# Attention loop of a hybrid decoder step on one core: projections moved ahead of the transposes in three of four steps

## The chip, the cores and the metric

The kernel is one program on one core of a Trainium2 chip. The metric is the device time of one execution in microseconds (us). The kernel before takes 2657.1 us, the median of three runs (2655.6, 2657.1, 2657.28).

TensorE (PE) multiplies matrices; its weight loads (PEld) are instructions of their own and overlap its matmuls. ScalarE (ACT) evaluates functions and copies, VectorE (DVE) does elementwise work and reductions, GpSimd (POOL) does the splitting of weights here, and SyncE (SP) issues most of the DMAs. Each engine runs its own instructions strictly in program order; the engines meet only at semaphores.

## The reference, cut to what matters

Two Griffin-style layers run over 1024 prompt tokens and 32 sample tokens (8 sequences of 4): one RG-LRU layer and one differential attention layer, each followed by a gated feed-forward block with a causal convolution. What the change touches is the attention layer, with 8 heads:

```python
kv = rmsnorm(x, kv_norm) @ w_kv                 # keys and values, also outputs
q  = (rmsnorm(x, norm_mix) @ w_q)               # per head two branches of 64
s  = einsum('bqhcd,bkhcd->bhcqk', q, k) * scale + bias   # causal, T5 bias
p  = softmax(s)
w  = p[:, :, 0] - lam * p[:, :, 1]              # difference of the two branches
o  = einsum('bhqk,bkhe->bqhe', w, v)
o  = rmsnorm(o, subln) * (1 - lam_init)
x  = x + o @ w_o
```

The sample tokens see 256 older keys and values besides, read from a paged cache.

## The kernel before, in words

All products are made as three matmuls of values split into a high and a low part, so that they keep float32 accuracy. The attention layer is one software pipeline, written out by hand: 64 **steps** `g`, which are 8 heads `h` times 8 query tiles of 128 rows (`t = g % 8`; `TILES` gives the order 0, 1, 7, 6, 2, 3, 5, 4 of the tiles). A tile `i` has `i + 1` key blocks, so steps with t = 2 and 3 are the large ones.

While a head's attention is computed, the projections (q, k, v) of the next head are made by the same engine between the pieces of attention. They are cut into **products** of three matmuls of 128x352 each (`fill`, lines 997, 999, 1001); eight products make a **chunk** (a third of the tokens of one 128-wide unit), three chunks a unit (`raw`), and nine products are done in each step. Chunks alternate between PSUM banks 0 and 1, so a chunk can start only when VectorE has taken out the chunk two before it (`raw_done`, lines 2209 and 2212). With nine products a step, a chunk begins after 6 products in the step t = 2, after 5 in t = 3, and so on down.

What TensorE does in a step, in this order:

- `scores(g)` (line 1029): query times keys of tile g, with 64-row matmuls in pairs, into banks 2 to 5; it waits until VectorE has read the scores before.
- `turn_weights(g - 2)` (line 1041): transposes of the combined softmax weights.
- `values(g - 3)` (line 1053): transposed weights times values.
- `sample_scores` in t = 0 (lines 1080, 1085) and `sample_output` in t = 4 (line 1112), both with 32-column matmuls; `sample_turn` in t = 5 (line 1121).
- `fill`, the nine products. In t = 2, 6 and 7 `ahead(g)` splits them into four and five, and between the two parts stand, in t = 2, `turn_values(h)` (lines 1065 and 1069: the values of the head turned, in three events) and `sample_weights(h)` (lines 1095, 1097), and in t = 6 and 7 `turn_output(h - 1, ...)` (line 1129).

The transposed weights, values and outputs land in PSUM banks that other engines empty. Banks 6 and 7 form a **ring**: `ring_order()` must list the events in the order in which TensorE makes them, each takes the bank of the one two before it, and has to wait for its reader (`open_event`). The weights of large tiles go to banks 3 and 5 instead (`beside_scores`), which the scores of large tiles need too: the scores in steps with g % 4 == 2 wait until the weights turned in the step before are read (`wait_weights_read`).

ScalarE does in a step: `weights_back(g - 2)` (line 1594, takes the turned weights out of PSUM), in t = 2 `values_out(h)` (issues the DMA of the values at line 1573 and takes the turned values out, lines 1576 and 1582), `exponentials(g)` (1603), `square_sum(g - 4)` (1612); in t = 4 `deviation(h - 1)` (1618, a square root, with a load of its table), `high_qk` (1542) and `sample_queries` (1556); at the head of t = 5 `sample_back(h)` (1665), whose result `sample_turn` waits for; at the head of t = 3 `sample_second(h)` (1654).

VectorE does in a step: `biased(g)` (2244: adds the bias, finds the minima), `output_rows(g - 3)` (2228, takes the result of `values(g - 3)` out of its ring bank), the chunks that are done, `combine(g - 1)` (2257, 2258, 2260), and in some steps the sample's operations. After the loop comes a tail written out by hand: the last heads' products end at step 56, steps 60 to 63 begin the output projection (`project`), and then `squares` (line 1180) follows in the ring.

Of the kernel before, what the change touches and what calls it, by code (L numbers as in the profile page):

```python
# [169 lines left out]
def filled(g):  # L170

    return LEAD if g < 0 else FIRST if g == 0 else min(16 + RATE * (g + 1), PRODUCTS)
# [4 lines left out]
    return (filled(g) - filled(g - 1)) // 3  # L177


def ahead(g):  # L180

    n = filled(g) - filled(g - 1)
    return n // 2 if g % 8 in (2, 6, 7) else 0


def beside_scores(g):

    return halves(g) == 2 and g < STEPS - 2
# [7 lines left out]
def ring_order():  # L196

    order = []
    for g in range(STEPS + 3):
        h, t = divmod(g, 8)  # L200
        if 2 <= g < STEPS + 2:
            order += [("w", g - 2, b) for b in range(halves(g - 2))]
        if g >= 3:
            order.append(("o", g - 3))
        if g < STEPS and t in (0, 4, 5):
            order.append((("scores", h), None, None, None, ("output", h), ("turned", h))[t])
        if g < STEPS and t == 2:
            order += [("v", h, 0), ("v", h, 1), ("v", h, 2), ("weights", h)]
        if g < STEPS and h and t >= 6:
            order.append(("ot", h - 1, t - 6))  # L210
        if g == STEPS - 1:
            order.append(("squares",))
    return order + [("ot", NH - 1, 0), ("ot", NH - 1, 1)]
# [33 lines left out]
def program(nc, I, O, S):  # L247
# [5 lines left out]
    with ExitStack() as ctx:  # L253
# [543 lines left out]
        def _(pe):  # L797
# [187 lines left out]
            def fill(n):  # L985

                for j in range(pos[0], min(pos[0] + n, PRODUCTS)):
                    q, k = divmod(j, KT)
                    m, c = divmod(q, NCH)
                    if j == 0:  # L990
                        wait_read(pe, A_A)
                    if q >= 2 and k == 0:
                        pe.wait_ge(raw_done, q - 1)
                    if c == 0 and k == 0:
                        pe.wait_ge(w_lo, U_A + 2 + m + 1)
                    s, cols = (U_A + m) % 2, slice(c * CH, (c + 1) * CH)
                    pe.matmul(PS[:, q % 2, 0:CH], WHI[:, s, k, :], XNH[:, k, cols],  # L997
                              start=(k == 0), stop=False)
                    pe.matmul(PS[:, q % 2, 0:CH], WLO[:, s, k, :], XNH[:, k, cols],  # L999
                              start=False, stop=False)  # L1000
                    last = pe.matmul(PS[:, q % 2, 0:CH], WHI[:, s, k, :], XNL[:, k, cols],  # L1001
                                     start=False, stop=(k == KT - 1))
                    if k == KT - 1:
                        last.then_inc(chunk_done, 1)
                pos[0] = min(pos[0] + n, PRODUCTS)
# [7 lines left out]
            def scores(g):  # L1013
                h, t = divmod(g, 8)
                i, p = tile_of(g), h % 2
                n = (i + 1) * P
                if g >= 4 and g % 4 == 2:

                    wait_weights_read(pe, g - 3)
                if t == 0:  # L1020
                    pe.wait_ge(qkl_done, 2 * h + 2)
                if g:
                    pe.wait_ge(ttr_done, 2 * g)
                for b in range(0, n, 512):
                    w = min(512, n - b)
                    for j, (q, k) in enumerate(((QHI, KHI), (QLO, KHI), (QHI, KLO))):
                        for c in range(2):
                            rows = slice(c * HD, (c + 1) * HD)
                            last = pe.matmul(PS[:, 2 + 2 * c + b // 512, 0:w],  # L1029
                                             q[p][rows, i * P:(i + 1) * P], k[p][rows, b:b + w],  # L1030
                                             start=(j == 0), stop=(j == 2))
                            if j == 2 and b + w == n:
                                last.then_inc(s_done, 1)
# [90 lines left out]
            def turn_output(h, half):  # L1124

                pe.wait_ge(on_done, h + 1)
                z = open_event("ot", h, half)
                for b in range(4):
                    last = pe.transpose(PS[:, z, b * P:(b + 1) * P], OQ[:, h % 2, 4 * half + b, :],
                                        IDENT[:, :])  # L1130
                last.then_inc(ev_done, 1)
# [22 lines left out]
            for g in range(STEPS):  # L1154
                h, t = divmod(g, 8)
                scores(g)
                if g >= 2:
                    turn_weights(g - 2)
                if g >= 3:
                    values(g - 3)  # L1160
                if t == 0:
                    sample_scores(h)
                if t == 4:
                    sample_output(h)
                if t == 5:
                    sample_turn(h)
                fill(ahead(g))
                if t == 2:
                    turn_values(h)
                    sample_weights(h)  # L1170
                if h and t >= 6:
                    turn_output(h - 1, t - 6)
                fill(filled(g) - filled(g - 1) - ahead(g))
                if g == STEPS - 4:
                    pe.wait_ge(raw_done, PRODUCTS // KT)
                if g >= STEPS - 4:
                    project(g - (STEPS - 4), 0, (0, 1))
            pe.wait_ge(sosq_done, 1)
            z = open_event("squares")
            pe.matmul(PS[:, z, 0:NH * TS], ONES[:, :], OSQ[:, :, :].rearrange("p h t -> p (h t)"),  # L1180
# [98 lines left out]
        def _(act):  # L1279
# [398 lines left out]
            for g in range(STEPS):  # L1678
                h, t = divmod(g, 8)
                if 0 < h < NH - 1 and t == 7:  # L1680
                    output_back(h - 1, 0)
                if g == STEPS - 1:
                    act.wait_ge(chunk_done, PRODUCTS // KT)
                    output_high(NH - 2, 0)
                if g >= STEPS - 5:
                    high_o(g - (STEPS - 5))
                if h > 1 and t == 0:
                    output_back(h - 2, 1)
                if t == 3:
                    sample_second(h)  # L1690
                if t == 5:
                    sample_back(h)
                if g >= 2:
                    weights_back(g - 2)
                if t == 2:
                    values_out(h)
                exponentials(g)
                if t == 1:
                    sample_exponentials(h)
                if g >= 4:  # L1700
                    square_sum(g - 4)
                if h and t == 4:
                    deviation(h - 1)
                if t == 4 and h + 1 < NH:
                    high_qk(3 * h + 3)
                    sample_queries(h + 1)
                if t == 6 and h + 1 < NH:
                    high_qk(3 * h + 4)
                    keys_out(h + 1)
                if g == STEPS - 1:  # L1710
                    high_o(NH - 3)
                if g == STEPS - 2:
                    act.wait_ge(osm_done, 1)
                    act.activation(OSQ[:, :, :], OSM[:, :, :], ACT.Square).then_inc(sosq_done, 1)
# [46 lines left out]
        def _(dve):  # L1761
# [598 lines left out]
            for g in range(STEPS):  # L2360
                h, t = divmod(g, 8)
                if g == STEPS - 1:
                    output_low(NH - 2, 0)
                if t == 1:
                    sample_biased(h)
                if t == 3:
                    sample_combined(h)
                if t == 6:
                    sample_rows(h)
                biased(g)  # L2370
                if g >= 3:
                    output_rows(g - 3)
                evac_chunks(chunks_by(g, portion(g)))
                if g:
                    combine(g - 1)
                if t == 0:
                    sample_biases(h)
                if t == 2:
                    sample_normalized(h)
                if h and t == 4:  # L2380
                    variance(h - 1)
                if h and t == 5:
                    scaled(h - 1)
                if g == STEPS - 2:
                    wait_event_read(dve, "turned", NH - 1)
                    dve.memset(CARRY[:, 5:6], 0.0).then_inc(osm_done, 1)
                evac_chunks(chunks_by(g, 2 * portion(g)))
                if g >= STEPS - 5:
                    low_o(g - (STEPS - 5))
            output_low(NH - 2, 1)  # L2390
            combine(STEPS - 1)
            output_rows(STEPS - 3)
            low_o(NH - 3)
# [204 lines left out]
```

## Time and profile before

| what | value |
|---|---|
| median of three runs | 2657.1 us |
| profiled execution, its own time | 2657.53 us |
| its span | 2655.4 us |
| PE busy | 2600.1 us (98%), 16892 matmuls |
| DVE / ACT / POOL busy | 1453.0 (55%) / 704.1 (27%) / 833.3 (31%) us |
| chain that ended last | PE 89%, DVE 6%, ACT 3% |

The profile is of one execution, which took 0.4 us more than the median of the three timed ones. A matmul's end is modelled, so the start times of consecutive matmuls are what shows its price: a product's three matmuls each start 0.16 us after the one before. The attention loop runs from the first scores at 1223.03 us to step 57 at 1655.52 us of the span, and the tail of the loop up to about 1712 us.

### The profile page before, as it was taken

How to read it: one execution, taken by the hardware profiler on the slowest of the kernel's cores; microseconds unless marked ns; L12 is line 12 of the kernel's file. 1: busy time of each engine (PE TensorE's matmuls, PEld its weight loads, DVE VectorE, ACT ScalarE, POOL GpSimd, SP SyncE). 2: the span in 40 equal slices, each digit the busy share in tenths (PEclk: the TensorE clock that was granted, in tenths of full speed). 3: DMA queues.
4: the chain of work that ended last, by engine and by line, in shares of the span. 5: the costliest groups of instructions: out<-in, count | busy, mean ns of one | idle time of the engine just before them, and what ended most of it. 6: DMA issues, size and time to landing. Idle time of an engine off the chain costs nothing.

```text
span 2655.4 us, 40398 instructions
## 1 busy us (share of the span) xinstructions
PE 2600.1 (98%) x16892; PEld 2539.0 (96%) x16892; DVE 1453.0 (55%) x2302; ACT 704.1 (27%) x1172; POOL 833.3 (31%) x458
## 2 busy tenths in 40 slices
PE   8899999999999999999999999899999999999997
PEld 8899999999999999998999998799999999999997
DVE  8766375444444445476556555636445544444448
ACT  5555031111111111124444444512111111111112
POOL 2332333233233233334333333023233323323321
PEclk9999999999999999999999999999999999999999
DMA  4111311111111111134233232311111111111112
GB/s 148 44 35 32 121 47 41 48 47 41 49 48 41 47 48 45 43 122 131 83 103 99 95 96 92 134 52 41 48 48 43 45 48 43 46 48 48 40 48 80
DMA packets 81922, 170.05 MB, mean 64 GB/s; under 512 B 9509, under 2 KB 47909, under 8 KB 81486
## 3 DMA queue, kind: packets, MB, share of 16 engines
q1 hardware_dynamic: 75790, 145.18, 17.2%
q10 hardware_dynamic: 5952, 22.30, 2.2%
q8 instruction: 133, 2.18, 0.3%
q14 instruction: 47, 0.39, 0.0%
HBM read 145.93 MB, written 26.23 MB: 65 GB/s over the span
## 4 chain that ended last, share of the span: by engine, by line
PE 89%; DVE 6%; ACT 3%; issue 1%; POOL 0%; DMA 0%; DVEq 0%; SPq 0%; ACTq 0%; POOLq 0%
PE psum L803 70%; PE psum L997 3%; PE psum L999 3%; PE psum L1001 3%; PE psum L1053 2%; PE psum L1029 2%; PE psum L1041 1%; PE psum L1233 1%; DVE line L1812 1%; DVE line L1772 1%; PE psum L1112 0%; DVE y L1964 0%; DVE xn_lo L1829 0%; DVE xn_lo L1972 0%; PE psum L1085 0%
## 5 line engine op out<-in xcount | busy, mean ns | idle before, releaser
L803 PE MATMUL psum<-xn_hi,w_hi 128*128 128x352 f32 x3024 | 655.9, 325 | 4.5 <-DVE xn_lo L1972 1.8
L803 PE MATMUL psum<-xn_lo,w_hi 128*128 128x352 f32 x3024 | 652.2, 323 | 0.0
L803 PE MATMUL psum<-xn_hi,w_lo 128*128 128x352 f32 x3024 | 651.5, 323 | 0.0
L693 POOL TENSOR_SCALAR w_hi<-w_raw 128x1024 fp32r<-128x1024 f32 x172 | 188.4, 1095 | 1445.8 <-PE psum L803 1343.6
L803 PEld LDWEIGHTS psum<-xn_hi,w_hi 128*128 128x128 f32 x3024 | 515.6, 189 | 8.0 <-POOL w_lo L697 2.9
L803 PEld LDWEIGHTS psum<-xn_lo,w_hi 128*128 128x128 f32 x3024 | 519.6, 188 | 0.0
L803 PEld LDWEIGHTS psum<-xn_hi,w_lo 128*128 128x128 f32 x3024 | 514.0, 188 | 0.0
L697 POOL TENSOR_TENSOR w_lo<-w_raw,w_hi 128x1024 fp32r<-128x1024 f32 x172 | 444.2, 2582 | 14.3
L1492 ACT ACTIVATE line<-line,columns 128x1072 f32<-128x1072 f32 x96 | 123.4, 1285 | 1057.3 <-DVE line L1795 1057.3
L1836 DVE TENSOR_TENSOR x<-psum,x 128x1056 f32<-128x1056 f32 x192 | 241.3, 1257 | 250.0 <-PE psum L803 246.0
L1790 DVE TENSOR_TENSOR line<-psum,inverse_rms 128x704 f32<-128x704 f32 x102 | 91.0, 892 | 463.4 <-PE psum L803 463.2
L1772 DVE SCALAR_TENSOR_TENSOR line<-line,columns,line 128x1072 f32<-128x1072 f32 (+1 forms) x112 | 189.2, 1689 | 111.8 <-ACT line L1492 100.6
L803 PE MATMUL psum<-h_hi,w_hi 128*128 128x352 f32 x1056 | 228.5, 324 | 0.1
L803 PE MATMUL psum<-h_lo,w_hi 128*128 128x352 f32 x1056 | 227.6, 323 | 0.0
L803 PE MATMUL psum<-h_hi,w_lo 128*128 128x352 f32 x1056 | 227.4, 323 | 0.0
L803 PEld LDWEIGHTS psum<-h_lo,w_hi 128*128 128x128 f32 x1056 | 181.3, 188 | 0.0
L803 PEld LDWEIGHTS psum<-h_hi,w_hi 128*128 128x128 f32 x1056 | 179.9, 189 | 0.4 <-DVE x L1836 0.4
L803 PEld LDWEIGHTS psum<-h_hi,w_lo 128*128 128x128 f32 x1056 | 179.3, 188 | 0.0
L997 PE MATMUL psum<-xn_hi,w_hi 128*128 128x352 f32 x528 | 177.3, 336 | 1.1 <-DVE raw L2212 1.1
L1001 PE MATMUL psum<-xn_lo,w_hi 128*128 128x352 f32 x528 | 169.7, 321 | 0.0
L999 PE MATMUL psum<-xn_hi,w_lo 128*128 128x352 f32 x528 | 169.5, 321 | 0.0
L753 POOL TENSOR_TENSOR w_raw<-w_raw,columns 128x1024 f32<-128x1024 f32 x24 | 52.7, 2195 | 267.7 <-PE psum L1001 233.8
(272 smaller groups left out, 2961.7 us busy)
## 6 DMA issues: line engine op xcount, KB each, us to landing
w_raw<-in_w SPq DMA_DIRECT2D x200, 512.0 KB, 3.5
k_pages<-in_cache_k SPq DMA_DIRECT2D x128, 64.0 KB, 2.1
v_pages<-in_cache_v SPq DMA_DIRECT2D x128, 64.0 KB, 2.2
scratch_line<-scratch_row ACTq DMA_DIRECT2D x1, 4608.0 KB, 21.0
x<-in_x SPq DMA_DIRECT2D x8, 528.0 KB, 8.5
scratch_x<-x ACTq DMA_DIRECT2D x1, 4224.0 KB, 12.7
out_k<-raw ACTq DMA_DIRECT2D x8, 528.0 KB, 2.7
out_v<-raw ACTq DMA_DIRECT2D x8, 528.0 KB, 3.5
```

What stands on the lines that cost most here:

```text
L693: pool.tensor_scalar(WHI[:, s], WRAW[:, s], 1.0, 0.0, ALU.mult, ALU.add).then_inc(w_hi, 1)
L697: pool.tensor_tensor(WLO[:, s], WRAW[:, s], WHI[:, s].bitcast(F32), ALU.subtract).then_inc(w_lo, 1)
L803: last = pe.matmul(PS[:, 3 * (a % 2) + c, 0:CH], w[:, s, k, :], r[:, c * CH:(c + 1) * CH], start=start and first, stop=stop and final)
L997: pe.matmul(PS[:, q % 2, 0:CH], WHI[:, s, k, :], XNH[:, k, cols], start=(k == 0), stop=False)
L999: pe.matmul(PS[:, q % 2, 0:CH], WLO[:, s, k, :], XNH[:, k, cols], start=False, stop=False)
L1001: last = pe.matmul(PS[:, q % 2, 0:CH], WHI[:, s, k, :], XNL[:, k, cols], start=False, stop=(k == KT - 1))
L1029: last = pe.matmul(PS[:, 2 + 2 * c + b // 512, 0:w], q[p][rows, i * P:(i + 1) * P], k[p][rows, b:b + w], start=(j == 0), stop=(j == 2))
L1053: last = pe.matmul(PS[:, z, 0:P], WTS[g % 2][:, b * P:(b + 1) * P], V[p][:, b, :], start=(b == 0), stop=(b == i))
L1492: act.activation(TMP[v][:, 0:m], Z[4 + v][:, 0:m], ACT.Identity, scale=w0, bias=wb).then_inc(q["tap_done"], 1)
L1772: step(dve.scalar_tensor_tensor(tmp[:, 0:n], src[:, j:j + n], taps[j], tmp[:, 0:n], MUL, ADD))
L1790: dve.tensor_tensor(line[:, hist:hist + c2].rearrange("p (c t) -> p c t", c=2), PS[:, b:b + 2, 0:CH], RINV[:, 0:c2].rearrange("p (c t) -> ...
L1836: dve.tensor_tensor(as_acc(x), acc(a), as_acc(x), ADD).then_inc(acc_free[a % 2], 1)
```

## The change

On TensorE, nine products stand directly behind `scores(g)` in the steps with g % 4 != 1, ahead of `turn_weights` and `values`; in the steps with g % 4 == 1 they stay behind. They are no longer split (`ahead` is gone). `turn_values(h)` goes from t = 2 to the very end of t = 1; `sample_weights(h)` stays in t = 2 and `turn_output` in t = 6 and 7, each now at the end of its step. On ScalarE `values_out(h)` goes from before the exponentials of t = 2 to the end of t = 1. On VectorE `output_rows` is made one step later for the same tile (g - 4 instead of g - 3), but at the head of the step, before `biased(g)`; after the loop, `output_rows(STEPS - 4)` stands behind `output_low(NH - 2, 1)`. `ring_order` follows.

```diff
-def ahead(g):
-
-    n = filled(g) - filled(g - 1)
-    return n // 2 if g % 8 in (2, 6, 7) else 0
...
         if g < STEPS and t in (0, 4, 5):
             order.append((("scores", h), None, None, None, ("output", h), ("turned", h))[t])
+        if g < STEPS and t == 1:
+            order += [("v", h, 0), ("v", h, 1), ("v", h, 2)]
         if g < STEPS and t == 2:
-            order += [("v", h, 0), ("v", h, 1), ("v", h, 2), ("weights", h)]
+            order.append(("weights", h))
...
                 h, t = divmod(g, 8)
                 scores(g)
+                if g % 4 != 1:
+                    fill(filled(g) - filled(g - 1))
                 if g >= 2:
                     turn_weights(g - 2)
                 if g >= 3:
...
                 if t == 5:
                     sample_turn(h)
-                fill(ahead(g))
-                if t == 2:
-                    turn_values(h)
-                    sample_weights(h)
-                if h and t >= 6:
-                    turn_output(h - 1, t - 6)
-                fill(filled(g) - filled(g - 1) - ahead(g))
+                if g % 4 == 1:
+                    fill(filled(g) - filled(g - 1))
                 if g == STEPS - 4:
                     pe.wait_ge(raw_done, PRODUCTS // KT)
                 if g >= STEPS - 4:
                     project(g - (STEPS - 4), 0, (0, 1))
+                if t == 1:
+                    turn_values(h)
+                if t == 2:
+                    sample_weights(h)
+                if h and t >= 6:
+                    turn_output(h - 1, t - 6)
...
                 if g >= 2:
                     weights_back(g - 2)
-                if t == 2:
-                    values_out(h)
                 exponentials(g)
                 if t == 1:
                     sample_exponentials(h)
                 if g >= 4:
                     square_sum(g - 4)
+                if t == 1:
+                    values_out(h)
...
                 if g == STEPS - 1:
                     output_low(NH - 2, 0)
+                if g >= 4:
+                    output_rows(g - 4)
                 if t == 1:
                     sample_biased(h)
...
                 biased(g)
-                if g >= 3:
-                    output_rows(g - 3)
                 evac_chunks(chunks_by(g, portion(g)))
...
             output_low(NH - 2, 1)
+            output_rows(STEPS - 4)
             combine(STEPS - 1)
             output_rows(STEPS - 3)
```

## Rows read from the trace of the kernel before

**Rows 1.** Stretches: length, busy us (instructions) by engine, PE clock, DMA share, GB/s.

```profile
1223.03:1655.52 432.49, 428.54 (x3490) 389.36 (x3490) 250.84 (x739) 200.41 (x558) 152.62 (x76) 1.00 0.31 96
1671.40:1678.30 6.90, 5.87 (x61) 5.11 (x62) 5.99 (x15) 5.98 (x16) 0.00 (x0) 0.51 0.01 4
```

**Rows 2.** Timeline of PE, t = 2 of head 4: start, length, instruction [idle before <-releaser].

```profile
1481.49 1.03 PE L1065 MATMUL psum<-ident,raw 128*128 128x128 f32 x8
1482.77 0.28 PE L1069 MATMUL psum<-ident,raw 128*32 128x128 f32 x1 [0.25 <-ACT v L1576]
1483.35 0.27 PE L1095 MATMUL psum<-ident,sample_probs 128*32 128x128 f32 x1 [0.29 <-ACT v L1576]
1483.46 0.38 PE L1097 MATMUL psum<-ident,sample_probs 128*128 128x128 f32 x2
```

**Rows 3.** Timeline of PE, step 1, where products follow scores directly.

```profile
1226.49 0.32 PE L1001 MATMUL psum<-xn_lo,w_hi 128*128 128x352 f32 x1
1226.74 0.39 PE L1029 MATMUL psum<-k_high,q_high 64*128 64x256 f32 x2
...
1227.08 0.28 PE L1029 MATMUL psum<-k_low,q_high 64*128 64x256 f32 x2
1227.29 0.43 PE L997 MATMUL psum<-xn_hi,w_hi 128*128 128x352 f32 x1
1227.56 0.32 PE L999 MATMUL psum<-xn_hi,w_lo 128*128 128x352 f32 x1
1227.72 0.32 PE L1001 MATMUL psum<-xn_lo,w_hi 128*128 128x352 f32 x1
```

**Rows 4.** Timeline of PE, a step t = 7.

```profile
1455.79 0.28 PE L1029 MATMUL psum<-k_low,q_high 64*128 64x128 f32 x2
1456.00 0.66 PE L1041 MATMUL psum<-ident,probs 128*128 128x128 f32 x4
1456.49 0.83 PE L1053 MATMUL psum<-v,w_t 128*128 128x128 f32 x6
1457.08 0.41 PE L997 MATMUL psum<-xn_hi,w_hi 128*128 128x352 f32 x1
```

**Rows 5.** Timeline of ACT, the same step.

```profile
1456.75 0.60 ACT L1594 ACTIVATE w_t<-psum 128x512 f32<-128x512 f32 x1 [3.33 <-PE psum L1041]
```

**Rows 6.** Timeline of PE, first scores of a step t = 2.

```profile
1476.70 0.50 PE L1029 MATMUL psum<-k_high,q_high 64*128 64x512 f32 x2
1478.29 0.33 PE L1041 MATMUL psum<-ident,probs 128*128 128x128 f32 x1
```

**Rows 7.** Timeline of DVE, the same step.

```profile
1479.72 1.22 DVE L2244 CUSTOM_DVE_ANT_0 probs<-psum,bias_strip 128x1024 f32<-128x1024 f32 x1
...
1481.07 0.52 DVE L2209 SCALAR_TENSOR_TENSOR raw<-psum,inverse_rms 128x352 f32<-128x352 f32 x1
```

**Rows 8.** Timeline of PE, steps t = 4 and t = 5.

```profile
1493.20 1.09 PE L1041 MATMUL psum<-ident,probs 128*128 128x128 f32 x8
...
1504.18 0.38 PE L1121 MATMUL psum<-ident,sample_out 128*128 128x128 f32 x2
```

**Rows 9.** Timeline of ACT, the same step t = 4 and the head of t = 5.

```profile
1496.53 1.28 ACT L1618 ACT_TABLE_LOAD   x1
1498.69 0.21 ACT L1618 ACTIVATE small<-small 128x8 f32<-128x8 f32 x1 [0.88 <-DVE small L2270]
...
1500.42 0.39 ACT L1665 ACTIVATE sample_out<-psum 128x256 f32<-128x256 f32 x1
```

**Rows 10.** Timeline of PE, steps 58 and 63.

```profile
1662.62 0.66 PE L1065 MATMUL psum<-ident,raw 128*128 128x128 f32 x4 [1.02 <-DVE o_q L2228]
...
1694.38 0.59 PE L1180 MATMUL psum<-o_sample_sq,ones 128*128 128x256 f32 x2
...
1697.44 0.60 PE L1041 MATMUL psum<-ident,probs 128*128 128x128 f32 x4
```

**Rows 11.** Timeline of DVE, `output_low` behind the loop.

```profile
1696.45 0.75 DVE L2350 SCALAR_TENSOR_TENSOR xn_lo<-psum,subln_scaled,xn_hi 128x512 fp32r<-128x512 f32 x1
```

## The prediction

> **What bounds the kernel now.** I read the table of busy times first: TensorE is busy for 98% of the span and 89% of the last chain is its own. In the stretches, the attention loop (1223.03 to 1655.52 us) shows TensorE busy for 428.54 of 432.49 us at full clock [rows 1]. So there are less than 4 us of plain idleness to win in the loop. VectorE (251 us) and ScalarE (200 us) have slack in sum; they count only where TensorE waits for one result. The heads repeat with one pattern, so I read one head in the timeline and multiply.
>
> The idleness sits mostly at one place, once per head: the turned values and the sample's weights [rows 2]. Eight transposes start at 1481.49, 0.11 apart (1.03 less the last one's 0.27, over 7), so the ninth could start at 1482.36 and starts at 1482.77: 0.41 lost, because its ring bank must first be read by ScalarE. The next could start at 1482.88 and starts at 1483.35: 0.47 lost.
>
> **The change part by part.** TensorE computes the same matmuls, so the price is in waits and in changes of matmul shape.
>
> *A, turned values at the end of t = 1, sample weights at the end of t = 2.* The three events of the values keep their two banks, so the 0.41 stays: ScalarE is idle there during the products, as it is now. The 0.47 goes: a whole step's work lies between. What could be late next is the normalising on VectorE; it follows the large `biased` and a small combination, and has all nine products (27 x 0.16 = 4.3) as cover. 7 heads x 0.47 = -3.3 us. Bounds 0 and -3.3.
>
> *B, products straight behind the scores of t = 2.* There a chunk starts after 6 products and needs VectorE to have emptied the chunk two before. VectorE gets to it only behind `biased`, whose second half runs 1479.72 to 1480.94 [rows 7]. Without the copy that now stands between, the chunk starts near 1480.88 and takes 0.52: it ends at 1481.40, that is 4.70 after the scores began at 1476.70 [rows 6]. TensorE reaches the chunk 1.59 (scores, rows 6) + 18 x 0.16 + 0.10 (the first product after scores, below) = 4.57 after that start. It is 0.15 to 0.2 early, and after a wait the weight load of the next matmul is exposed, by about 0.1 as at any restart [rows 3]. 0.3 x 7 = +2.0 us. Bounds 0 and +4 (0.6 a head, were the copy still in front). In the other steps the boundary lies behind fewer products of a step whose forerunner was emptied earlier, or `biased` is shorter, so nothing waits. The queue behind this wait is TensorE's whole rest of the step.
>
> *C, turned output right behind the values in t = 7.* `turn_weights`, `values` and `turn_output` are three consecutive ring events of one step, so the third needs the bank of the first. ScalarE starts to read the four turned blocks 0.75 after the first transpose (1456.00 to 1456.75) and takes 0.60 [rows 4, 5]: free at +1.35 to +1.40. TensorE gets there at 4 x 0.11 + 6 x 0.10 = +1.05 to +1.10. So far four or five products stood between. 0.3 x 6 heads (1 to 6) = +1.7 us. Bounds 0 and +3. In t = 6 the tile before has five blocks (+1.5 against +1.15), in t = 2 the single transpose is read early, so both are free.
>
> *D, ScalarE's work comes 4.4 us later in each changed step.* Its `weights_back` waits for transposes that now follow the products, and everything queued behind it shifts: exponentials, in t = 4 the table load, square root, `high_qk`, the sample's queries, and then `sample_back`, for which TensorE's `sample_turn` waits in t = 5. Counted from the first transpose of t = 4 (1493.20): the table load ends at 1497.81, +4.61; from the square root to the end of `sample_back` it is 1498.69 to 1500.81, 2.12 [rows 9]. Together +6.73. TensorE needs from the same transpose to `sample_turn` 1504.18 - 1493.20 = 10.98 [rows 8] less the products that now stand ahead (27 x 0.16 + 0.2 for the two changes of shape = 4.5): +6.45. So a wait of 0.3 in heads 1 to 6 (head 0 has no square root): +1.7 us. Upper bound: if VectorE's variance is as late as now (the 0.88 of rows 9 comes back), ScalarE ends at +7.6, the wait is 1.2, +7 us. Lower bound 0. The variance depends on work of the step before, so I take it as in time. The exponentials of the other steps also come later, but their weights are turned two steps on, with 432.49 / 57 = 7.6 us a step [rows 1].
>
> *E, changes of matmul shape.* Scores directly followed by products show 0.21 and then 0.27 instead of 0.16 [rows 3]; scores followed by transposes show 0.21 and 0.05 more in the four transposes (0.49) [rows 4]. Products to scores cost 0.25 instead of 0.16 [rows 3], values to products nothing (1457.08 is on time, rows 4), and I take the same 0.09 for anything full-size before scores. So a step turned round is 0.05 dearer: 6 a head. Against that, in t = 0 and 4 the 32-column sample matmuls are now followed by 64-row scores, one change of shape instead of two; that is in no row. Between no gain and one whole change (0.2, the sum of rows 3's parts) I take 0.15 each. 6 x 0.05 - 2 x 0.15 = 0. Bounds -0.1 and +0.3 a head: -0.7 to +2 us.
>
> The rule on this in the Trainium skill is in TensorEngine Tiling (Array Packing), Key Properties: a change of tiling mode drains TensorE. Taken alone it counts 20 changes a head before and 18 after and makes the step orders otherwise equal; at the 0.2 of the scores' edges that would be -0.4 a head. Rows 3 against rows 4 show that the neighbour matters too.
>
> *F, steps 56 to 63 and the tail.* In step 57 the turned values now come before the scores of step 58, and their second event waits for `output_rows`, as in rows 10 (1.02 now; I estimate 0.4, and 0.7 for the ninth transpose, since ScalarE is still at the step's exponentials). The scores of 58 come about 2 us later, but steps 58 to 60 hang on the chain exponentials, `sample_second`, `sample_combined`, `biased`, and ScalarE no longer has `values_out` in front of the exponentials: about even, bounds -1 and +1.5. Where it gets worse is `squares`. Its ring bank is that of `output_rows(60)`, which now comes behind `output_low` (ends 1697.2 now, about 0.7 earlier after the change because VectorE no longer waits for output events in steps 61 and 62) [rows 11]. So `squares` goes from 1694.38 to about 1697, and with the projection behind it the next transposes from 1697.44 [rows 10] to 1698.7: +1.3. What follows is TensorE-bound, so it stays. With some of the first part I take +1.5; bounds 0 and +3.5.
>
> *DMAs.* The values' output is issued a step earlier, key and value pages of the next head up to 4.4 us later; SyncE reaches those waits only behind the next weight load, and their readers are most of a head away: nothing. GpSimd's low parts of the keys lose up to those 4.4 us of their lead of more than a step: nothing; if not, the first scores of each head would wait.
>
> Sum: -3.3 + 2.0 + 1.7 + 1.7 + 0 + 1.5 = +3.6 us on 2657.53, the profiled execution, so 2661.1. That execution is 0.4 above the median, so I say 2661.
>
> **The rivals.**
>
> *R1, slower: ScalarE's queue becomes the bound in t = 4 and 5.* Place: `sample_turn`. For it: the margin in D is a fraction of 1 us out of 6.5, and the square root was the last thing waited for in every head that I read. Against: the variance gets its inputs earlier relative to the new place. Decides from the moment that the square root starts more than about 0.3 later than its table load ends. Price up to 1.2 x 6 = 7 instead of 1.7: 2661 + 5.5 = 2666.5.
>
> *R2, slower: the low clock.* In 1671.40 to 1678.30 the PE clock is 0.51, which is 1.2 GHz instead of 2.4, behind the waits of steps 58 to 60; it cost half of the 5.87 busy us, 2.9 [rows 1]. The new wait at `squares` is about as long. One more such stretch of half that length costs 1.5 to 3: 2663.5.
>
> *R3, faster: the waits B to D don't appear.* A stays (-3.3), F is even, and the more even work of steps 57 to 60 spares the low stretch (-2.9) as well: 2651. For it: B, C and D are each only 0.3. Against: three independent chains would all have to be misjudged to the same side, and the tail's idleness comes from dependences that the change does not shorten.
>
> *R4, the drain rule alone:* E gives -2.8 instead of 0, time 2658.3, no measurable change.
>
> *R5, the change doesn't do what it says:* the order is meant to group matmuls of one number format. Values to products is on time to 0.01 [rows 4], so a change of format costs nothing and grouping by it gains nothing. This is part of my forecast.
>
> **Chances.** A measurement of this kernel tells 0.2%, 5.3 us, from no change; so faster is below 2651.8 and slower above 2662.4. Forecast 0.47 (of it 0.15 above 2662.4), R1 0.2 (all slower but 0.03), R2 0.08 (0.05 slower), R3 0.13 (0.1 faster), R4 0.12 (same). Faster 0.10, slower 0.37, same 0.53. Range: the forecast with the bounds of B to F, up to R1 and down to near R3: 2654 to 2668.
>
> **What would show it.** Right: in TensorE's waits, `sample_weights` (L1095) no longer waits, the ninth transpose (L1069) still does, and three new waits of 0.2 to 0.4 appear: L997 for VectorE's L2209 in t = 2, L1129 for ScalarE's L1594 in t = 7, L1121 for ScalarE's L1665 in t = 5; `squares` starts 2 to 3 us later. From one head to the next it takes 0.2 to 0.5 us more than now (the sum of A to E, over 7). Wrong: heads shorter than now by over 0.3; a wait of over 1 us at L1121; waits at the scores (L1029), which would mean that VectorE's lateness in t = 3 behind `sample_combined` reaches the next step; or a clock below 1 inside the loop.

## The result and the profile after

The changed kernel takes **2661.2 us** (median of 20 runs, 2660.58 to 2663.35), the kernel before in the same session 2657.62 us (20 runs, 2655.6 to 2658.83). The ratio is 1.0014, with a 95% interval of 1.0008 to 1.0021: 3.6 us slower, of which the interval leaves 2.1 to 5.6, so most of it lies below the 0.2% (5.3 us) named in the prediction: by that measure no change, though the interval leaves out zero. The forecast was 2661.

First the page of the profiled execution (its own time is 2662.4 us, 1.2 above the median): its span, busy times and last chain.

```profile
span 2660.5 us, 40398 instructions
PE 2601.2 (98%) x16892; PEld 2543.4 (96%) x16892; DVE 1443.1 (54%) x2302; ACT 700.0 (26%) x1172; POOL 834.6 (31%) x458
PE 88%; DVE 6%; ACT 4%; issue 1%; POOL 0%; DMA 0%; DVEq 0%; SPq 0%; ACTq 0%; POOLq 0%
```

As many matmuls as before, and 1.1 us more busy time: TensorE's work is the same, its gaps and changes of shape are not. Next the waits of TensorE in the attention loop (1224 to 1660 us): who waited for whom, us in total, times, the longest.

```profile
PE psum L1065 <- ACT v L1575: 1.8, 7, 0.3
PE psum L1117 <- ACT sample_out L1664: 1.7, 6, 0.3
PE psum L1125 <- ACT w_t L1593: 1.3, 6, 0.4
```

The old wait at the ninth transpose (L1065) is still there, the one at the sample's weights is gone, and two new ones have come, at `sample_turn` (L1117) and at `turn_output` (L1125). The third predicted one is not in this list; it is found below. In the tail of the loop (1655 to 1715 us) the same list begins:

```profile
PE psum L1179 <- DVE o_q L2227: 3.2, 1, 3.2
PE psum L1091 <- DVE sample_probs L2304: 2.7, 1, 2.7
PE psum L1025 <- DVE minima L2243: 1.8, 1, 1.8
```

And three stretches with the columns of [rows 1]: the loop, and the two stretches of the tail at the lower clock.

```profile
1224.05:1659.63 435.58, 430.72 (x3490) 393.73 (x3489) 239.70 (x736) 196.49 (x558) 154.30 (x78) 1.00 0.31 96
1675.90:1679.30 3.40, 3.39 (x24) 3.12 (x28) 3.33 (x11) 2.70 (x6) 0.00 (x0) 0.50 0.01 2
1699.80:1703.20 3.40, 3.02 (x13) 2.55 (x12) 0.48 (x1) 1.19 (x3) 0.00 (x0) 0.50 0.00 0
```

The loop takes 435.58 us instead of 432.49 [rows 1]: +3.1. From step 57 to the first product behind the attention layer it is 68.60 us against 68.30: +0.3. The rest of the 5.1 us between the two spans, 1.0 ahead of the loop and 0.7 behind the layer, lies in code that the change doesn't touch. Loop and tail together, +3.4, agree with the +3.6 of the medians.

To place it I take each step's length, from the start of its scores to the start of the next scores, the mean of the heads 1 to 6 (after the change, step 7 takes 7.58 in five of them and 7.86 in head 4):

| step | 0 | 1 | 2 | 3 | 4 | 5 | 6 | 7 | head |
|---|---|---|---|---|---|---|---|---|---|
| before | 7.79 | 6.88 | 9.47 | 6.32 | 8.20 | 8.12 | 8.06 | 7.22 | 62.06 |
| after | 7.66 | 8.36 | 7.94 | 6.37 | 7.98 | 8.62 | 8.12 | 7.63 | 62.69 |
| e1 | 7.79 | 8.29 | 7.60 | 6.31 | 8.20 | 8.12 | 8.06 | 7.22 | 61.59 |
| e4 | 7.67 | 8.30 | 7.66 | 6.36 | 7.99 | 8.15 | 8.12 | 7.24 | 61.49 |
| e9 | 7.66 | 8.34 | 7.60 | 6.31 | 7.99 | 8.13 | 8.03 | 7.22 | 61.28 |
| e10 | 7.67 | 7.91 | 7.60 | 6.32 | 7.99 | 8.13 | 8.03 | 7.23 | 60.87 |

Now the places themselves, as timelines (start, length, instruction, idle time before it and its releaser). The end of step 1 of head 4, on TensorE:

```profile
1478.72 1.03 PE L1061 MATMUL psum<-ident,raw 128*128 128x128 f32 x8
1480.01 0.28 PE L1065 MATMUL psum<-ident,raw 128*32 128x128 f32 x1 [0.25 <-ACT v L1575]
1480.22 0.50 PE L1025 MATMUL psum<-k_high,q_high 64*128 64x512 f32 x2
```

These are the transposes of [rows 2] in their new place. The ninth could start at 1479.60 and starts at 1480.01: the 0.41 has moved with them unchanged, and the scores follow directly where 0.47 was lost.

Step 2, the chunk's border behind the sixth product, on TensorE, and the chunk before it on VectorE:

```profile
1484.46 0.32 PE L995 MATMUL psum<-xn_hi,w_lo 128*128 128x352 f32 x1
1484.62 0.32 PE L997 MATMUL psum<-xn_lo,w_hi 128*128 128x352 f32 x1
1484.96 0.43 PE L993 MATMUL psum<-xn_hi,w_hi 128*128 128x352 f32 x1
1485.23 0.32 PE L995 MATMUL psum<-xn_hi,w_lo 128*128 128x352 f32 x1
```

```profile
1484.39 0.52 DVE L2208 SCALAR_TENSOR_TENSOR raw<-psum,inverse_rms 128x352 f32<-128x352 f32 x1
```

The steps between matmuls are 0.16, then 0.34 and 0.27: 0.29 is lost. VectorE ends at 1484.91, 4.69 after the scores began at 1480.22 (predicted: 4.70), and TensorE goes on 0.05 later. No wait is printed, since the modelled end of the matmul before (1484.94) covers the gap. Only the starts show it. It comes in the heads 1 to 6; in head 0 step 2 takes 6.55 in the change and 6.54 in e4, where this wait is mended.

Steps 4 and 5, on ScalarE and on TensorE:

```profile
1502.93 1.28 ACT L1617 ACT_TABLE_LOAD   x1
1504.23 0.21 ACT L1617 ACTIVATE small<-small 128x8 f32<-128x8 f32 x1
1504.34 1.04 ACT L1541 ACTIVATE q_high<-raw 128x1024 fp32r<-128x1024 f32 x1
1505.95 0.38 ACT L1664 ACTIVATE sample_out<-psum 128x256 f32<-128x256 f32 x1
```

```profile
1504.24 1.95 PE L1049 MATMUL psum<-v,w_t 128*128 128x128 f32 x16
1506.48 0.41 PE L1117 MATMUL psum<-ident,sample_out 128*128 128x128 f32 x2 [0.28 <-ACT sample_out L1664]
```

The square root starts at the end of its table load; the 0.88 of [rows 9] is gone. So R1's condition (a square root over 0.3 late) did not come, in no head of the loop, and the wait is the small one.

The end of step 7 of the same head, on TensorE:

```profile
1524.87 0.60 PE L1037 MATMUL psum<-ident,probs 128*128 128x128 f32 x4
1525.30 0.83 PE L1049 MATMUL psum<-v,w_t 128*128 128x128 f32 x6
1526.58 0.63 PE L1125 MATMUL psum<-ident,o_q 128*128 128x128 f32 x4 [0.45 <-ACT w_t L1593]
```

It is the three ring events in a row; this head has the longest of the six waits (its step 7 takes 7.86), the others have 0.2. Last the tail, on TensorE and on VectorE:

```profile
1695.40 0.60 PE L1125 MATMUL psum<-ident,o_q 128*128 128x128 f32 x4
1699.18 0.67 PE L1179 MATMUL psum<-o_sample_sq,ones 128*128 128x256 f32 x2 [3.18 <-DVE o_q L2227]
1699.50 0.57 PE L1137 MATMUL psum<-xn_hi,w_hi 128*128 128x352 f32 x1
1699.87 0.49 PE L1139 MATMUL psum<-xn_hi,w_lo 128*128 128x352 f32 x1
1700.16 0.49 PE L1141 MATMUL psum<-xn_lo,w_hi 128*128 128x352 f32 x1
```

```profile
1698.09 0.75 DVE L2349 SCALAR_TENSOR_TENSOR xn_lo<-psum,subln_scaled,xn_hi 128x512 fp32r<-128x512 f32 x1 [0.91 <-ACT xn_hi L1635]
1698.75 0.28 DVE L2227 COPY o_q<-psum 128x128 f32<-128x128 f32 x1
```

`squares` (L1179) waits for the row copy that stands behind `output_low` (L2349), and right behind it the products come 0.29 apart instead of 0.16: the granted clock is 0.50 there, 1.2 GHz.

### The profile page after: what moved, and what is told of

Its sections match the earlier page's. It is cut to its first block, busy times and chain, and to the rows that moved or that the text cites. A ratio compares the mean times of both kernels' runs of the same rounds, so it can differ in the third digit from the quotient of the medians.

```text
span 2660.5 us, 40398 instructions
## 1 busy us (share of the span) xinstructions
PE 2601.2 (98%) x16892; PEld 2543.4 (96%) x16892; DVE 1443.1 (54%) x2302; ACT 700.0 (26%) x1172; POOL 834.6 (31%) x458
## 4 chain that ended last, share of the span: by engine, by line
PE 88%; DVE 6%; ACT 4%; issue 1%; POOL 0%; DMA 0%; DVEq 0%; SPq 0%; ACTq 0%; POOLq 0%
PE psum L799 70%; PE psum L993 4%; PE psum L997 3%; PE psum L995 3%; PE psum L1025 2%; PE psum L1049 2%; PE psum L1232 1%; PE psum L1037 1%; DVE line L1811 1%; DVE line L1771 1%; ACT probs L1602 0%; DVE y L1963 0%; DVE xn_lo L1828 0%; ACT w_t L1593 0%; ACT L1617 0%
## 5 line engine op out<-in xcount | busy, mean ns | idle before, releaser
L1776 DVE SCALAR_TENSOR_TENSOR line<-line,columns,line 128x1024 f32<-128x1024 f32 x100 | 131.2, 1312 | 3.5
```

The source lines that it names most:

```text
L1776: dve.scalar_tensor_tensor(dst[:, 0:SEQ], src[:, hist:hist + SEQ], taps[hist], tmp[:, 0:SEQ], MUL, ADD)
```

## The experiments

The theory: one wait of 0.47 a head is saved, three small ones come and one large one at `squares`, each through one edit of order, and the changes of shape cancel. The rivals: ScalarE's queue as a bound (R1), the clock (R2), a drain at each change of shape alone (R4), number formats (R5). Differences below are to the kernel before in the same session: 2657.24 us for e1 to e4 (33 runs), 2657.38 for the others (15 runs); the change itself stands at +3.6.

| run | median us (runs) | to before | ratio, 95% |
|---|---|---|---|
| e1 | 2654.63 (11) | -2.6 | 0.999, 0.9981 to 0.9999 |
| e2 | 2658.09 (11) | +0.9 | 1.0004, 0.9995 to 1.0013 |
| e3 | 2658.44 (11) | +1.2 | 1.0005, 0.9996 to 1.0014 |
| e4 | 2651.95 (11) | -5.3 | 0.998, 0.9971 to 0.9989 |
| e5 | 2661.84 (1) | +4.5 | one run |
| e6 | 2660.85 (1) | +3.5 | one run |
| e9 | 2651.05 (11) | -6.3 | 0.9977, 0.9968 to 0.9986 |
| e10 | 2647.4 (5) | -10.0 | 0.9963, 0.995 to 0.9977 |

**e1, the turned values alone.** The kernel before, with nothing but part A: no products are moved.

```diff
                 fill(ahead(g))
-                if t == 2:
-                    turn_values(h)
-                    sample_weights(h)
                 if h and t >= 6:
                     turn_output(h - 1, t - 6)
                 fill(filled(g) - filled(g - 1) - ahead(g))
+                if t == 1:
+                    turn_values(h)
+                if t == 2:
+                    sample_weights(h)
...
-                if t == 2:
-                    values_out(h)
                 exponentials(g)
...
+                if t == 1:
+                    values_out(h)
```

> The kernel before with part A alone: turned values (and ScalarE's values_out) at the end of t = 1, sample_weights at the end of t = 2; products, VectorE and everything else as before. Theory 'waits': only the 0.47 us wait ahead of the sample's weights goes, 7 heads: t = 1 and t = 2 together shorter by 0.45 to 0.5 us a head, time 3 us below the kernel before (about 2654.5), no other step longer. Rival 'order does not matter' (the loop is PE-bound and the wait is filled elsewhere): no difference in the steps. Rival 'tail': the turned values come before the large scores of step 58 and cost 1 to 2 us there, so 2656.

Steps 1 and 2 take 15.88 us together instead of 16.35, and no other step changes: -0.47 a head, or -3.3 in seven, and the whole loop is 3.4 shorter (429.10 us). The time falls by 2.6, and the interval reaches up to 0.9999, so the step lengths carry this result. Part A is the main gain in the change. The wait of 2.9 us for `sample_probs` in step 58 is already in this kernel's tail (it is 0.7 before and 2.7 in the change), so it belongs to A.

**e2, `sample_back` early.** The change, with ScalarE's `sample_back` ahead of the table load instead of behind it.

```diff
-                if t == 5:
-                    sample_back(h)
...
                     values_out(h)
+                if t == 4:
+                    sample_back(h)
                 if h and t == 4:
```

> The changed kernel with ScalarE's sample_back in t = 4, behind square_sum and ahead of the square root, instead of at the head of t = 5. Theory 'waits' (part D): TensorE's wait at sample_turn in t = 5 (L1117) vanishes in heads 1 to 6; step t = 5 goes from 8.63 to about 8.18 us; 6 x 0.45 = 2.7 us less than the changed kernel: 2658.5. Rival: the longer t = 5 comes from the change of matmul shapes, then it stays at 8.63.

Step 5 goes from 8.63 to 8.14, and no other step of the loop moves; TensorE's waits in the loop are now these:

```profile
PE psum L1065 <- ACT v L1575: 1.8, 7, 0.3
PE psum L1125 <- ACT w_t L1593: 1.3, 6, 0.4
```

0.49 in six heads is 2.9; the time fell by 2.7 against the change. D is shown, and it costs more than the 0.28 printed beside the wait: the start of the transposes is 0.45 late (sixteen matmuls from 1504.24 at 0.11 end at 1506.03, and 1506.48 is the start).

**e3, `output_rows` early.** The change, with the row copy of step 60 in step 63, as before, not behind `output_low`.

```diff
                 biased(g)
+                if g == STEPS - 1:
+                    output_rows(g - 3)
...
             output_low(NH - 2, 1)
-            output_rows(STEPS - 4)
```

> The changed kernel, but VectorE takes out the rows of step 60 behind biased(63), as the kernel before does, instead of behind output_low at the end. Theory 'waits' (part F): the 3.2 us wait at squares (L1179) goes to under 0.5; if the low-clock stretch at 1699.8 us was caused by it, that goes too (another 1.5 us): 3 to 4.5 us less than the changed kernel, 2657 to 2658. Rival: something else on VectorE's chain (low_o, output_low) is late next and TensorE waits at the projection instead: 1 us or less gained.

The tail's timeline on TensorE, and its one stretch at the lower clock:

```profile
1695.07 0.60 PE L1179 MATMUL psum<-o_sample_sq,ones 128*128 128x256 f32 x2
1696.73 0.43 PE L1137 MATMUL psum<-xn_hi,w_hi 128*128 128x352 f32 x1 [1.06 <-DVE xn_lo L2341]
1696.99 0.32 PE L1139 MATMUL psum<-xn_hi,w_lo 128*128 128x352 f32 x1
```

```profile
1675.10:1678.50 3.40, 3.34 (x24) 3.08 (x28) 3.33 (x12) 2.70 (x6) 0.00 (x0) 0.50 0.01 2
```

`squares` no longer waits, the projection behind it now waits 1.06 for the low part, and the stretch at 1699.8 is gone: its products are 0.16 apart. The wait counted 3.18 - 1.06 = 2.1, the clock half of 3.02 busy us, 1.5; from step 57 to the first product behind the layer it is 65.78 us against 68.60, 2.8 less, and by the medians the edit is worth 2.4. That is under the 3 to 4.5 expected, and the rival's late low part is there, as the wait of 1.06. The clock's fall at this place goes with the wait in all ten traces: the change, e2, e5 and e6 have a wait of 3.18 at `squares` and 3.4 us at 0.50 that begin within 1.3 us of its end; before, e1, e3, e4, e9 and e10 have neither.

**e4, all four mended.** e2 and e3, and three products of step 2 and two of step 7 put back behind the values.

```diff
-                if g % 4 != 1:
-                    fill(filled(g) - filled(g - 1))
+                n = filled(g) - filled(g - 1)
+                behind = n if g % 4 == 1 else min(n, {2: 3, 7: 2}.get(t, 0))
+                fill(n - behind)
...
-                if g % 4 == 1:
-                    fill(filled(g) - filled(g - 1))
+                fill(behind)
```

> The changed kernel with all four waits mended: in t = 2 six products ahead and three behind the values (B), in t = 7 seven and two (C), sample_back ahead of the square root (D), output rows of step 60 behind biased(63) (F). Theory 'waits': per head B 0.28, C 0.30, D 0.45 less, in the tail 3 us or more: 2 + 1.8 + 2.7 + 3.5 = 10 us below the changed kernel, 2651, and so 6 us below the kernel before. Rival: waits move on to the next late result; then half of it, 2656.

The time is 5.3 below before, 8.9 below the change. Step 2 lost 0.28 (7.94 to 7.66) in six heads, step 7 0.34 (7.58 to 7.24) in five and 0.62 in head 4; 1.7 + 2.3 + e2's 2.7 + e3's 2.4 = 9.1, a little less than the 10 expected. So the four waits add up, and no new one came in their place. One wait is left in the loop, the old one:

```profile
PE psum L1065 <- ACT v L1575: 1.8, 7, 0.3
```

Set against e1, e4 also tells what the products' new places are worth once their waits are gone: the loop takes 428.40 us against e1's 429.10, a head 61.49 against 61.59. That is 0.7 us; what the change gains in the loop is nearly all in A.

**e5, a product behind the sample's matmuls.** The change, with one of the nine products of steps 0 and 4 at the end of the step, which puts the change of shape back.

```diff
+                behind = n if g % 4 == 1 else min(n, {0: 1, 4: 1}.get(t, 0))
+                fill(n - behind)
...
+                fill(behind)
```

> The changed kernel, but in t = 0 and t = 4 one of the nine products stands behind the sample's 32-column matmuls instead of ahead of the transposes. Read from the start times of the steps alone. Theory 'edges cost' (part E, and the drain rule): the 32-column matmuls are again followed by full-size ones and these by 64-row scores, one change of shape more: t = 0 goes from 7.66 to 7.8 to 7.9 us and t = 4 from 7.98 to 8.15 to 8.25. Rival 'the gain in t = 0 and 4 came from something else' (the products' place behind the scores): both stay within 0.03.

In step 0 of head 4, first the change, then e5, both on TensorE (the `x4` are the last four of the sixteen, which start in fours):

```profile
1470.86 1.05 PE L1081 MATMUL psum<-k_pages,q_padded 128*32 128x256 f32 x16
1471.51 0.40 PE L1081 MATMUL psum<-k_pages,q_padded 128*32 128x256 f32 x4
1471.84 0.39 PE L1025 MATMUL psum<-k_high,q_high 64*128 64x256 f32 x2
```

```profile
1470.53 0.40 PE L1081 MATMUL psum<-k_pages,q_padded 128*32 128x256 f32 x4
1470.86 0.43 PE L993 MATMUL psum<-xn_hi,w_hi 128*128 128x352 f32 x1
1471.13 0.32 PE L995 MATMUL psum<-xn_hi,w_lo 128*128 128x352 f32 x1
1471.29 0.32 PE L997 MATMUL psum<-xn_lo,w_hi 128*128 128x352 f32 x1
1471.55 0.39 PE L1025 MATMUL psum<-k_high,q_high 64*128 64x256 f32 x2
```

A product between 32-column and 64-row matmuls costs 0.27 + 0.16 + 0.26 = 0.69 instead of 0.48. Step 0 is 0.19 longer, step 4 0.21, as expected; it is one execution, but the same in every head from 1 to 6. So one more change of shape is 0.2 here. The 32-column matmuls are left at the same price either way: their fours start 0.22 apart (three in 1471.51 - 1470.86), and what follows the last four starts 0.33 behind them, 0.11 more, be it the scores (1471.84) or the product (1470.86). Step 5's wait vanished too (8.15): the tail end of step 4 gave ScalarE the time it lacked. This agrees with D.

**e6, products between the transposes and the values.** The change, with four products of steps 0 and 3 between these two.

```diff
                     turn_weights(g - 2)
+                fill(between)
                 if g >= 3:
```

> The changed kernel, but in t = 0 and t = 3 four of the nine products stand between the turned weights and the values, so that the number format of the matmuls changes twice more in the step while the shape (full size) doesn't. Read from the start times of the steps. Theory 'a change of format is free' (R5): t = 0 stays at 7.66 and t = 3 at 6.37, within 0.03. Rival 'grouping by format is what a reordering can win': each extra pair of changes costs 0.1 or more.

Step 0 takes 7.67 against 7.66, step 3 6.37 against 6.37, with two more changes of number format in each. In the timeline of step 0 the values follow the products in beat, 0.16 on:

```profile
1468.79 0.32 PE L997 MATMUL psum<-xn_lo,w_hi 128*128 128x352 f32 x1
1468.95 1.06 PE L1049 MATMUL psum<-v,w_t 128*128 128x128 f32 x8
```

Grouping by format gains nothing here (R5), as forecast; it is one execution.

**e9, products ahead in two steps only.** e2 and e3 again, and products ahead only where they save a change of shape. (`GAP` is a switch that e10 turns on.)

```diff
+GAP = False
...
-                if g % 4 != 1:
+                if t in (0, 4):
                     fill(filled(g) - filled(g - 1))
...
-                if g % 4 == 1:
-                    fill(filled(g) - filled(g - 1))
+                if t not in (0, 4):
+                    fill(filled(g) - filled(g - 1) - (1 if GAP and t == 1 else 0))
```

> The mended kernel with the products ahead of the transposes only in t = 0 and t = 4, behind everything in the others (turned values, sample weights and turned outputs still at the end of their steps). Theory 'waits and edges': t = 0 and t = 4 keep 7.66 and 7.98; t = 2, 3, 6, 7 are 0.05 shorter than in the mended kernel (7.60, 6.31, 8.06, 7.2); a head takes 61.25 us against 61.48, so 1.6 us less than the mended kernel: 2650.3. Rival 'ring': a wait comes back at the turned outputs or in t = 5, and it is no faster than 2652.

The head is 0.21 shorter than e4's: steps 2, 3, 6 and 7 are 0.02 to 0.09 shorter (expected 0.05 each), step 1 is 0.04 longer. The loop is 1.6 shorter than e4's (426.84 us), as expected, and 2.3 shorter than e1's; no wait came back in it. The time is 0.9 below e4's, or 1.0 by each one's own session, instead of 1.6. The intervals of the two overlap, so the step lengths carry this.

**e10, a product inside the turned values.** e9, with one of step 1's nine products between the second and the third event of the turned values, to fill the 0.41.

```diff
-GAP = False
+GAP = True
...
                     last.then_inc(ev_done, 1)
+                fill(min(1, filled(8 * h + 1) - filled(8 * h)))
                 z = open_event("v", h, 2)
...
                 if t not in (0, 4):
-                    fill(filled(g) - filled(g - 1) - (1 if GAP and t == 1 else 0))
+                    fill(filled(g) - filled(g - 1) - (1 if GAP and t == 1 and h < NH - 1 else 0))
```

> As the kernel with only two steps ahead, and one of the nine products of t = 1 stands between the second and the third event of the turned values. Theory 'waits': the 0.41 us wait at the ninth transpose (L1065's group) in heads 0 to 6 goes, since a product takes 0.48: t = 1 from 8.29 to 7.88, 7 x 0.41 = 2.9 us less: 2647.4. Rival: the wait isn't ScalarE's read of the bank alone and half of it stays.

```profile
1471.30 1.03 PE L1064 MATMUL psum<-ident,raw 128*128 128x128 f32 x8
1472.09 0.41 PE L996 MATMUL psum<-xn_hi,w_hi 128*128 128x352 f32 x1
1472.34 0.33 PE L998 MATMUL psum<-xn_hi,w_lo 128*128 128x352 f32 x1
1472.50 0.32 PE L1000 MATMUL psum<-xn_lo,w_hi 128*128 128x352 f32 x1
1472.66 0.27 PE L1069 MATMUL psum<-ident,raw 128*32 128x128 f32 x1
```

The ninth transpose starts 0.16 behind the product, with no wait, and the loop lists none at all. Step 1 is 0.42 shorter in each of seven heads, 2.9, and the loop 2.7 (424.11 us). The time is 3.7 below e9's, with no execution of the one among those of the other, and 10.0 below the kernel before. What it has beyond the 2.7 is not shown to be the product's: the profiled tail of e10 has 3.4 us at the low clock, e9's 10.2. It is the fastest version.

## Why the prediction came out

The sum was right, +3.6 as measured. Two of its parts were wrong, to opposite sides: the loop got 3.1 instead of 2.1, the tail 0.3 instead of 1.5. The places and causes of the loop's waits were foreseen; that the two errors cancel to 0.2 is luck. By the prediction's own signs, a head was to take 0.2 to 0.5 more; it takes 0.63 more.

- **A, right.** -0.47 a head, and the 0.41 went along with the values (e1).
- **B, right in place, cause and size.** 0.29 a head, in six heads and not seven: 1.7 for 2.0. VectorE's end was predicted within 0.01 us, counting from the scores. Expected as a printed wait, it is in no list.
- **C, right in mechanism, a little small.** 0.2 printed and 0.34 in the step's length (7.24 to 7.58), 0.62 in head 4: 2.3 for 1.7.
- **D, the mechanism right, the term too small.** The step that failed is "a wait of 0.3 in heads 1 to 6: +1.7". The printed wait was 0.28; the step lost 0.49 (e2), so +2.9. The prediction had added 0.1 for the restart behind a wait in B, and not in D. R1 did not come: its variance was in time.
- **E, one part too small.** The four ordinary steps are each 0.02 to 0.06 dearer (e4 against e1), 0.05 as taken. The two with sample matmuls gained 0.13 and 0.22 instead of 0.10 each, since the change of shape saved is worth the whole 0.2 (e5) and not 0.15. That makes -0.15 a head instead of 0, outside the bound of -0.1. The Trainium skill says that a change of tiling mode drains TensorE (TensorEngine Tiling (Array Packing), Key Properties). The trace agrees where a change is added (0.2, e5). R4's -0.4 did not come: the order of the shapes costs too, and e9 gains by moving products back. A to E by these sizes make about +0.5 for a head and the steps show +0.6; the rest of 0.1 sits in steps 1 and 2 and was not pursued.
- **F, the named place right but too cheap, the rest wrong.** `squares` waited 3.2 us for the predicted copy. It starts 4.8 us later than before, of which 4.1 is the shift that step 57 already has (1655.52 to 1659.63), so in the end it is 0.7 late and not 2.6. Still, against this kernel's own course the wait and the clock behind it are worth 2.4 (e3), not 1.3. The step that failed is "about even, bounds -1 and +1.5" for steps 58 to 60, together with the steps behind them, on which the prediction is silent. The scores of step 63 start 34.62 us behind those of step 57 before and 31.68 after: 2.9 us were given back, although `sample_weights` now waits 2.7 in step 58 instead of 0.7. Of this 1.2 is in step 62, where TensorE waited before:

```profile
PE psum L1053 <- DVE o_sample L2334: 1.2, 1, 1.2
```

  In every trace with the new order this wait is gone and step 62 takes 4.94 to 4.98 us; before and in e1 it takes 6.14 and 6.15. That is a gain of the order that the prediction lacks. The other 1.8 lie in steps 57 to 60. One part of it can be seen: 3.4 us at the lower clock there instead of the 10.2 that the trace of before shows in 1664.6 to 1668.0 and 1671.4 to 1678.3. How much of the 1.8 is due to the order and how much to the execution was not separated; e4 with the same order there had 10.2 us again.
- **R2 came in part**: a stretch of 3.4 us at half the clock, directly behind the new wait. R3 needs the three waits to stay away, and they came; e4, where they are taken out by hand, lands near its 2651 (2651.95), but not by its sum, since the tail's low clock is there in full.

In e4 the tail's clock was as bad as before, and the time was still 5.3 below before. e4, e9 and e10 have one order in the tail, and it takes 66.63, 68.33 and 65.81 us in their traces, with 10.2, 10.2 and 3.4 us at the low clock. So one execution's tail can differ by 2.5 us from another's, which is as much as the terms of F, while the loop's steps repeat to 0.1 us.

## What to carry to other kernels

When an engine is busy 99% of a loop, moving work costs or gains only through single waits and changes of shape. List for each move the ring bank or result that is read next, who reads it and what stands before that reader in its queue, and count both sides from one common start; that gave the three new waits of the loop within 0.2 us in every head but one. Price a wait by the starts of the instructions around it, not by the idle time printed. Split the fill work and put single pieces of it where a bank has to come back: one product in the right place (e10, 2.9 us in seven heads) was worth more than moving the products ahead in six steps of a head (0.7 us in the loop, e4 against e1) or in two (2.3, e9 against e1).

## What the runs showed of the hardware that was not expected

- The loss from a wait is larger than the printed one: 0.28 printed and 0.45 by the starts at L1117, 0.25 and 0.41 at L1065, nothing printed and 0.29 at the chunk's border.
- Leaving 32-column matmuls costs 0.11, whether 64-row or full-size ones follow: the last four `sample_scores` start 0.33 ahead of the next matmul, where their fours are 0.22 apart (e5). A full-size product put between them and the 64-row scores costs 0.2 more than its own three beats.
- The low clock came with the 3.2 us wait at `squares` (0.50 from 1699.8 on) in the four traces that have it, and stayed away where the only wait near is the 1.06 behind `squares` (e3). The 19 waits listed in the loop, none over 0.45, left it at 1.00. The longest single wait does not decide it: in the trace of before, waits of 1.02 and 0.67 (1661.6 to 1664.1) were followed by 0.50 from 1664.6 on, and one of 1.38 that ended at 1696.36 was not.
